# Three groups' squares summed on VectorE, and their sums over channels moved by half a projection tile

## What is computed

```python
proj = u @ w_in
z, xbc, dt = jnp.split(proj, [D_INNER, D_INNER + CONV_DIM], axis=-1)
...   # convolution over tokens, SiLU, the state recurrence: y
y = y.reshape(b, L, D_INNER) * jax.nn.silu(z.astype(jnp.float32))
yg = y.reshape(b, L, SSM_GROUPS, D_INNER // SSM_GROUPS)
yg = yg * lax.rsqrt(jnp.mean(yg * yg, axis=-1, keepdims=True) + EPS)
y = (yg.reshape(b, L, D_INNER) * norm_w.astype(jnp.float32)).astype(u.dtype)
return y @ w_out, new_conv, final.astype(u.dtype)
```

## Time and profile before

| what | us |
|---|---|
| median of 3 runs | 970.09 (969.07 to 970.49) |
| the profiled execution | 970.61 |
| its span, first to last instruction | 968.8 |
| TensorE busy (matmul) | 947.6, 98% |
| VectorE busy | 543.9, 56% |
| ScalarE busy | 478.6, 49% |
| GpSimd busy | 318.3, 33% |
| mean granted TensorE clock | 0.996 of full speed |

### The profile page before, as it was taken

How to read it: one execution, slowest core, us unless ns; L and a number is a source line. 1 busy time by engine, 2 the same in 40 slices (tenths; PEclk the granted TensorE clock), 3 DMA queues, 4 the chain that set the end, 5 groups by cost and what they waited for, 6 DMA issues and landing times.

```text
span 968.8 us, 18472 instructions
## 1 busy us (share of the span) xinstructions
PE 947.6 (98%) x7288; PEld 878.8 (91%) x7288; DVE 543.9 (56%) x1412; ACT 478.6 (49%) x943; POOL 318.3 (33%) x257
## 2 busy tenths in 40 slices
PE   9999999999999999999999999999999999999988
PEld 8998899989998999979988889998899988998877
DVE  4234421534234421557687669856688566886772
ACT  6335612464235613477346656256562565626762
POOL 3442234233242244226433234422344222442400
PEclk9999999999999999999999999999999999999989
DMA  7522222332224222112435634255432663427303
GB/s 210 180 73 93 61 88 81 122 109 88 88 73 151 87 87 75 64 24 78 122 92 145 187 85 130 85 156 175 110 122 68 169 170 104 142 65 212 90 12 104
DMA packets 144614, 105.91 MB, mean 109 GB/s; under 512 B 10754, under 2 KB 135860, under 8 KB 144464
## 3 DMA queue, kind: packets, MB, share of 16 engines
q1 hardware_dynamic: 134536, 100.19, 34.4%
q10 hardware_dynamic: 9992, 4.54, 1.9%
HBM read 91.99 MB, written 16.79 MB: 112 GB/s over the span
## 4 chain that ended last, share of the span: by engine, by line
PE 88%; DVE 8%; issue 2%; ACT 1%; DMA 1%; POOL 0%; SPq 0%; DVEq 0%; ACTq 0%; POOLq 0%
PE pp L1262 22%; PE pp L1264 21%; PE pp L1263 21%; PE pS L1372 2%; PE pO L1596 2%; PE pS L1603 2%; PE pO L1592 2%; PE pT_ L1582 2%; PE pO L1419 1%; PE pO L1418 1%; DVE s_in L2246 1%; PE pO L1543 1%; PE pS L1515 1%; PE pS L1553 1%; PE pT_ L1394 1%
## 5 line engine op out<-in xcount | busy, mean ns | idle before, releaser
L699 POOL TENSOR_TENSOR w_lo_buf<-w_raw_buf,w_hi_buf 128x512 fp32r<-128x512 f32 x214 | 274.8, 1315 | 470.5 <-ACT w_hi_buf L775 290.2
L1262 PE MATMUL pp<-h_hi,w_hi_buf 128*128 128x280 f32 (+2 forms) x1248 | 377.0, 302 | 2.1 <-DVE rb L1968 2.0
L1264 PE MATMUL pp<-h_hi,w_lo_buf 128*128 128x280 f32 (+2 forms) x1248 | 362.6, 291 | 0.0
L1263 PE MATMUL pp<-h_lo,w_hi_buf 128*128 128x280 f32 (+2 forms) x1248 | 362.2, 290 | 0.0
L1262 PEld LDWEIGHTS pp<-h_hi,w_hi_buf 128*128 128x128 f32 x1248 | 234.8, 188 | 11.2 <-issue 8.0
L1263 PEld LDWEIGHTS pp<-h_lo,w_hi_buf 128*128 128x128 f32 x1248 | 234.9, 188 | 4.6 <-issue 4.1
L1264 PEld LDWEIGHTS pp<-h_hi,w_lo_buf 128*128 128x128 f32 x1248 | 235.1, 188 | 0.0
L775 ACT ACTIVATE w_hi_buf<-w_raw_buf 128x2048 fp32r<-128x2048 f32 (+1 forms) x55 | 104.1, 1892 | 34.2 <-DMA w_raw_buf<-in_w_ssm_in 23.6
L1774 DVE TENSOR_TENSOR x<-x,pp 128x272 f32<-128x272 f32 (+3 forms) x128 | 56.4, 441 | 84.4 <-PE pp L1264 83.8
L1262 PE MATMUL pp<-og_hi,w_hi_buf 128*128 128x280 f32 (+2 forms) x256 | 75.5, 295 | 2.7 <-DVE x L1774 1.1
L1264 PE MATMUL pp<-og_hi,w_lo_buf 128*128 128x280 f32 (+2 forms) x256 | 74.4, 291 | 0.0
(11 more groups left out here) (348 smaller groups left out, 1611.1 us busy)
## 6 DMA issues: line engine op xcount, KB each, us to landing
w_raw_buf<-in_w_attn_in SPq DMA_DIRECT2D x16, 1024.0 KB, 5.1
w_raw_buf<-in_w_ssm_in SPq DMA_DIRECT2D x16, 1024.0 KB, 5.7
w_raw_buf<-in_w_attn_out SPq DMA_DIRECT2D x8, 1024.0 KB, 5.2
s_in<-in_state_ssm SPq DMA_DIRECT2D x32, 256.0 KB, 4.2
out<-s_in SPq DMA_DIRECT2D x32, 256.0 KB, 3.1
w_raw_buf<-in_w_ssm_out SPq DMA_DIRECT2D x8, 1024.0 KB, 6.6
seg<-a_scratch SPq DMA_DIRECT2D x12, 512.0 KB, 5.0
w_raw_buf<-in_w_attn_in SPq DMA_DIRECT2D x8, 512.0 KB, 6.2
```

The lines of the kernel that those rows point to most:

```text
L699: ins = pool.tensor_tensor(low_buf(n)[:, piece], raw[n % RAW_SLOTS][:, piece], high_buf(n)[:, piece].bitcast(F32), ALU.subtract)
L1262: pe.matmul(dst, hi[:, k, cols], a_hi[:, k, tk], start=(k == 0), stop=False)
L1263: pe.matmul(dst, hi[:, k, cols], a_lo[:, k, tk], start=False, stop=False)
L1264: mm = pe.matmul(dst, lo[:, k, cols], a_hi[:, k, tk], start=False, stop=(k == depth - 1))
```

## The change

For the groups 0 to 2 sum_y becomes one product per part. Before it, a new VectorE step add_squares adds the squares: tiles 0 and 1 plus tiles 2 and 3 in one instruction (two rows of columns), then tile 0 plus tile 1. The last group keeps its four products. The places in the orders change as well: the sum of part 0 comes after bc tile 1 half 1 instead of before it, the halo transposes and the sum of part 1 half a tile of x later each, final_state half a tile later; the adds stand on VectorE behind the evacuation of bc tile 1 half 0 (part 0) and behind the first tap of the next group's first convolution (part 1), in front of which the evacuation of x tile 0 half 0 is put. On ScalarE the copy of the final state comes behind the SiLU of the next group's first convolution.

```diff
+            def copy_final(g):
+                act.wait_ge(fs_tr, g + 1)
+                act.activation(sT[0][:, :], pS[:, 1, :], ACT.Copy).then_inc(fs_ready, 1)
...
                 silu_conv(g, 0)
                 if g:
+                    copy_final(g - 1)
                     high_y(g - 1, 0)
...
-                act.wait_ge(fs_tr, g + 1)
-                act.activation(sT[0][:, :], pS[:, 1, :], ACT.Copy).then_inc(fs_ready, 1)
+            copy_final(GROUPS - 1)
...
             def sum_y(g, part):
                 tk = part_of(g, part)
                 pe.wait_ge(xw_done, UNITS * (g + 1))
+                if g + 1 < GROUPS:
+                    pe.wait_ge(sqy_added, 2 * g + part + 1)
+                    pe.matmul(pS[:, part, 0:tk.stop - tk.start], ones[:, :], xc[:, 0, tk],
+                              start=True, stop=True).then_inc(ssy_done, 1)
+                    return
                 for t in range(HEADS):
...
+                if g:
+                    project("x", s, 0, 0)
                 pe.wait_ge(ci_in, 48 * (g + 1))
...
                 if g == 0:
                     tile_of("bc", s, 1)
-                project("x", s, 0, 0)
+                    project("x", s, 0, 0)
+                project("x", s, 0, 1)
                 if g:
                     sum_y(g - 1, 1)
-                project("x", s, 0, 1)
+                project("x", s, 1, 0)
                 if g:
                     final_state(g - 1)
-                tile_of("x", s, 1)
+                project("x", s, 1, 1)
                 project("x", s, 2, 0)
...
                     project("bc", s + 1, 1, 0)
                     part_b(g, UNITS - 1)
+                    project("bc", s + 1, 1, 1)
                     sum_y(g, 0)
-                    project("bc", s + 1, 1, 1)
...
+            def add_squares(g, part):
+                tk = part_of(g, part)
+                dve.wait_ge(sqy_ready, 8 * g + 4 * part + 4)
+                link(dve.tensor_tensor(xc[:, 0:2, tk], xc[:, 0:2, tk], xc[:, 2:4, tk], ALU.add))
+                dve.tensor_tensor(xc[:, 0, tk], xc[:, 0, tk], xc[:, 1, tk], ALU.add).then_inc(sqy_added, 1)
...
+                    conv_in(g, 2, 0)
                     conv_tap(g, 0, 0)
-                    conv_in(g, 2, 0)
+                    add_squares(g - 1, 1)
                     conv_tap(g, 0, 1)
...
                     gate_y(g, 0)
                     conv_in(g + 1, 1, 0)
+                    add_squares(g, 0)
                     new_state(g, UNITS - 1)
```

More of the change, by code:

```diff
@@ L406, in build @@
             sem(n) for n in ("yz_ready", "sqy_ready", "ssy_done", "rg_ready", "yn_ready"))
+        sqy_added = sem("sqy_added")
         fs_tr, fs_ready, fs_out = sem("fs_tr"), sem("fs_ready"), sem("fs_out")
```

## The result

The changed kernel takes **981.62 us** (median of 4 runs, 979.17 to 983.87) against 969.58 us before (4 runs, 968.2 to 970.49): a ratio of 1.012, 95% interval 1.0109 to 1.0132. It is 12 us slower where 7.3 us faster was forecast. The profiled execution took 983.87 us, the longest of the four; its span is 982.1 us, 13.3 more than before.

The account below looks back on a forecast made before the run. TensorE was taken to bound the kernel: 970.6 us profiled, minus 8.2 for the cut, plus 3 x 0.3 for waits, gave 963.3; the median, 0.5 lower, made 962.8 us. Own range 961.2 to 965.0; 8-in-10 range 960.4 to 966.5.

Parts of the forecast that it names:

- The bound: Around the first change of group TensorE is busy 79.89 of 80 us, so whatever is taken off it there shortens the kernel.
- The size of the cut: Three of four products dropped per token part in three groups: 2.75 us a group, 8.2 us in all, bounds 7.3 to 8.9.
- the prediction's own range: Range of the forecast time from the cut's bounds and waits of 0 to 0.8 us a group: 961.2 to 965.0 us.
- The search for the first late thing: Second half of the forecast: at the changes of group, look for whatever arrives too late for the earlier TensorE.
- the squares: VectorE's squares before sum 0 end at 575.95 us, adds at 577.5, TensorE asks at 578.5: 1 us to spare.
- VectorE's dense stretch: VectorE from norm_y at 590.34 us to low_y, hardly a hole; slack 0.7 us now, 0.3 to 0.4 us after.
- the collision: Two-input VectorE adds beside GpSimd's pieces: each add may cost from nothing to 1.3 us more; mean waits 0.2 us a group.
- The wait for VectorE at the sums: TensorE waiting at the sums for adds lengthened by GpSimd's pieces: mean of all such waits put at 0.2 us a group.
- The out slab and the copy: ScalarE's later final-state copy delays the out slabs' fetch; second group's slack falls from 3.6 to 0.4 us; 0.1 us a group.
- The rival "slower": Copy, out slab, split_lo run 3 us or more beyond slack in each group, TensorE then at half clock: 979 us; chance 0.04.
- The prediction's own sign of being wrong: One product costing TensorE clearly less than 0.6 us, or waits of over 1 us at each change of group.
- The clock: TensorE at half clock after a long wait, as in the tail's last group sum: some 2 us on top of the wait.

Follow-up runs that it names:

- the one with the early slab: Changed kernel, but GpSimd splits the next group's first x slab before its last decay of the state instead of behind it; 962.0 us, repeated at 962.59 us.
- the kernel with the old places: Changed kernel with adds, single products and early slab split, but TensorE's order as before the change and part 1's adds heading VectorE's group work; 978.39 us.
- run 3: No run of this name occurs in the text given, so no change or time can be stated for it.

## Why the prediction was wrong, point by point

- **The bound** (TensorE, 79.89 of 80 us) was right. It was read as room to cut, and that was the trap. A stretch without a hole says that hardly anything is late, not how much slack there is.
- **The size of the cut** was right: 8.2 us by the sum, bounds 7.3 to 8.9, and 7.2 to 7.8 measured with the defect out of the way. That includes the 0.7 us of the adds. The products alone show in the stretches: 33.38 us with four of them and 30.61 with one and no adds, 2.77 us in a group where 2.75 was forecast. (The upper end of the prediction's own range adds up to 970.1 - 7.3 + 2.4 = 965.2, not 965.0; nothing hangs on it.)
- **The search for the first late thing** is the step that failed. It followed the squares, VectorE's dense stretch and the out slabs. It never asked what TensorE needs for the x tile behind the moved sum. Its row was in hand: the pieces 576.48 5.00 were used only as what the adds collide with. That they end at 581.48, and that TensorE takes up x at 581.58, was never set side by side, and a wait for this slab was priced at nothing. With it the forecast would have been: no slack; TensorE asks 0.55 us (halo transposes) and 1.9 us (products) sooner; wait 2.45 us in each group. The kernel without adds measured 2.42. With three falls of the clock at the 1.55 us measured since, it would have been 970.6 - 8.2 + 3 x (2.45 + 1.55) = 974.4 us; that kernel took 974.98. So near a hit is in part luck: its clock fell only twice there, and some 1.7 us came in the out phase behind the second change, which this sum doesn't have.
- **The rest of the loss is the collision** in the other direction. The adds were expected to suffer from GpSimd's pieces, and did: 1.66 and 1.54 us where 0.95 and 0.56 were worked out. But GpSimd suffered too: its decay took 1.60 us for 1.04 in the second group, its four pieces 6.01, 5.73 and 5.74 for 5.00; with the adds cut to one column both are back (1.04 and 4.98). So the slab came still later: the x product starts 8.22, 8.51 and 8.02 us after the state product, for 581.58 - 574.38 = 7.2 before, and the waits became 2.65 (with 0.57 more at the sum ahead of it), 3.73 and 3.25 us. The prediction's rule for this came from the Trainium skill (SBUF — State Buffer, section Who interferes with whom): a VectorE instruction with two SBUF inputs and a GpSimd instruction that reads SBUF shut each other out, and the order of issue decides which of them waits. The lengths on both engines agree with that; I had used it for one of them.
- **The wait for VectorE at the sums** was sized at 0.2 us a group, 0.6 in all. It measured 1.6: 0.57 at part 0 and 0.75 at part 1 of the first group, 0.27 at part 1 of the second. All three are gone once the slab is split early. The slack was thinner than worked out, though: the adds of part 0 then end at 576.77 and the sum starts at 577.17, 0.4 us later, where 1 us was forecast.
- **The out slab and the copy** were second-order, as forecast. In the second group of the kernel after the out slab's last piece ends at 733.07 and the first out product starts at 733.17, the 0.10 us of a release again, so the 0.4 us of slack forecast there were used up. With the x slab early 1.6 us are left (719.10 to 720.68), and the copy ahead of the SiLU changed nothing.
- **The rival "slower"** had the right mechanism, a slab late behind the earlier TensorE and the clock at half speed after the wait, and nearly the right time (979). It looked at the wrong slab, needed 3 us beyond a slack of 0.4, and so had a chance of 0.04. The prediction's own sign of being wrong, waits of over 1 us at each change of group, is what came.
- **The clock** was priced at 2 us a fall from the tail; the falls measured 1.54, 1.56 and 2.63 us.

The ledger of the 22.0 us between the profiled executions of the kernel after and of the one with the early slab: waits for the slab 2.65 + 3.73 + 3.25 = 9.6; waits at the sums 1.6; half clock 5.7; together 16.9 of the 18.1 in the three stretches. About 1.2 us there is not assigned. Outside them, the out phase behind the second change takes 1.8 us more, with one low_y step of VectorE at 4.78 us beside GpSimd's pieces (2.69 in the kernel with the early slab; 4.81 with the slab late and no adds, so the adds aren't its cause):

```profile
730.72 4.78 DVE L2172 TENSOR_TENSOR y_lo<-z,y_hi 128x384 fp32r<-128x384 f32 x4
```

and 1.5 us stand in the last group, where the clock of the kernel after fell once more. What was not tried: the kernel after with only GpSimd's share of the collision removed. That the waits are 0.2 to 1.3 us longer than 2.42 is shown by the edit that takes the adds out; that this part comes by way of GpSimd's lengthened work is read from the traces.

## What to carry to other kernels

Ahead of a cut on the engine that bounds a kernel, list everything that it takes up in the next few microseconds, with the moment at which each becomes ready and whether that moment moves along with the cut. What hangs on an event ahead of the cut stays where it is, and a product without a wait in the trace may have been released at that very moment: no view of waits showed it here, only the end of the producer beside the start of the user, 0.10 us apart as in every real wait for the slab. And look at the order of the engine that produces it: here the mend was to put one step of GpSimd ahead of another that was waiting anyway, and it turned 12 us lost into 7.5 us gained.

## What was not expected of the hardware

- The same wait of 2.42 us, before the same instruction and with the same work around it, was followed by half clock in two of three groups and by full clock in the third. The price of a fall was 1.55 us there. In the kernel after, the fall behind the second group's wait of 3.73 us cost the same, behind the third's of 3.25 us 2.6. In the kernel with the old places a wait of 2.70 us brought no fall and one of 2.68 us did.
- The lower clock isn't tied to the wait itself: in the kernel after it is granted 1.00 up to the end of the first wait (582.16) and 0.50 from 582.4 on, in the third group it is 0.50 within the wait already (828.0 to 828.6), and in the third group of the kernel without adds TensorE works at full clock for 1.2 us (822.49 to 823.72) before it falls.
- Products that do nothing pay for themselves in such a wait: 2.9 us of them in the last group's wait of 3.5 us gained 1.8 us, and four more sums a group in the slab's wait gained 4.0. The Trainium skill (TensorE: Matmul & The Clock Gate, section What's actually happening) says that activity releases the throttle and that the throttled state is the default; the traces agree, with 1.00 granted in the filled stretches and 0.50 behind each wait of the kernel after.
- A VectorE instruction and GpSimd's pieces beside it lengthened both: 0.56 us became 1.54 on VectorE, and 5.00 became 6.01 on GpSimd. The same add of part 1, VectorE in the kernel after, in the first and the second group, once beside GpSimd's work and once alone:

```profile
590.09 1.29 DVE L2157 TENSOR_TENSOR xc<-xc 128x160 f32<-128x160 f32 x1
...
713.45 0.33 DVE L2157 TENSOR_TENSOR xc<-xc 128x160 f32<-128x160 f32 x1
```
